# The input LayerNorm of a transformer layer: scale and shift moved behind the transposes, residual rows made later, on one Trainium2 core

## What is computed

```python
def layer_norm(x, g, b):
    mu = jnp.mean(xf, axis=-1, keepdims=True)
    var = jnp.mean(jnp.square(xf - mu), axis=-1, keepdims=True)
    return (xf - mu) * lax.rsqrt(var + LN_EPS) * g + b

h = layer_norm(x, ln_in_g, ln_in_b)
qa, ka, va, qb, kb, vb, ga, gb = jnp.split(h @ w_in, pts, axis=-1)
ya = diff_attention(qa, ka, va, ...)     # branch A, 8 heads
yb = window_attention(qb, kb, vb, ...)   # branch B
merged = sigmoid(ga) * (ya @ w_branch_a) + sigmoid(gb) * (yb @ w_branch_b)
h = layer_norm(ALPHA * h + merged @ w_out, ln1_g, ln1_b)
h = layer_norm(ALPHA * h + square(relu(h @ w_ff1)) @ w_ff2, ln2_g, ln2_b)
```

## Time and profile before

| | |
|---|---|
| median of three runs | 1929.89 us |
| profiled execution, its time | 1934.76 us |
| its span, first to last instruction | 1932.9 us |
| PE busy | 1835.3 us, 95% of the span |
| DVE, ACT, POOL busy | 906.2, 609.7, 504.3 us |
| first matmul of a projection | at 40.09 us |
| first scores of branch A | at 82.93 us |
| branch A, period of a head | 59.5 us |

### The profile page before, as it was taken

How to read it: one execution, slowest core, us unless ns; L and a number is a source line. 1 busy time by engine, 2 the same in 40 slices (tenths; PEclk the granted TensorE clock), 3 DMA queues, 4 the chain that set the end, 5 groups by cost and what they waited for, 6 DMA issues and landing times.

```text
span 1932.9 us, 24565 instructions
## 1 busy us (share of the span) xinstructions
PE 1835.3 (95%) x9174; PEld 1508.9 (78%) x9174; DVE 906.2 (47%) x2051; ACT 609.7 (32%) x1336; POOL 504.3 (26%) x306
## 2 busy tenths in 40 slices
PE   3899999999989998999999999999999999999996
PEld 2777777777768887888888878788888888888884
DVE  7266666676655554111432365434343333334347
ACT  4355555555545555220222221211111111111104
POOL 5111111110113333222221210533222333333224
PEclk9999999999989998999999999999999999999998
DMA  4511111111111100124322350221111111121102
GB/s 161 199 52 32 46 34 34 44 46 33 32 38 31 31 23 23 51 70 138 120 80 66 98 196 1 76 73 48 54 43 43 43 43 43 44 72 47 43 0 87
DMA packets 143109, 117.88 MB, mean 61 GB/s; under 512 B 23285, under 2 KB 129965, under 8 KB 143021
## 3 DMA queue, kind: packets, MB, share of 16 engines
q1 hardware_dynamic: 133804, 112.51, 18.4%
q10 hardware_dynamic: 9216, 4.20, 0.8%
HBM read 99.87 MB, written 21.53 MB: 63 GB/s over the span
## 4 chain that ended last, share of the span: by engine, by line
PE 63%; DVE 4%; ACT 2%; issue 1%; POOL 0%; POOLq 0%; DVEq 0%
PE bank L474 20%; PE bank L475 20%; PE bank L476 20%; ACT mix L866 2%; PE bank L498 1%; DVE mix L1213 1%; PE bank L510 1%; DVE small L1218 1%; DVE res L1095 1%; DVE y_lo L1060 0%; DVE y_lo L1075 0%; ACT y_hi L744 0%; DVE res L1344 0%; ACT y_hi L731 0%; POOL res L964 0%
## 5 line engine op out<-in xcount | busy, mean ns | idle before, releaser
L474 PE MATMUL bank<-hT_hi,w_hi 128*128 128x512 f32 x1312 | 528.7, 403 | 11.6 <-ACT res L750 5.1
L475 PE MATMUL bank<-hT_lo,w_hi 128*128 128x512 f32 x1312 | 516.9, 394 | 0.0
L476 PE MATMUL bank<-hT_hi,w_lo 128*128 128x512 f32 x1312 | 516.7, 394 | 0.0
L959 POOL TENSOR_TENSOR w_lo<-w_raw,w_hi 128x1024 fp32r<-128x1024 f32 x67 | 161.6, 2411 | 710.6 <-ACT w_hi L725 710.5
L474 PEld LDWEIGHTS bank<-hT_hi,w_hi 128*128 128x128 f32 x1312 | 249.6, 190 | 71.9 <-issue 10.2
L476 PEld LDWEIGHTS bank<-hT_hi,w_lo 128*128 128x128 f32 x1312 | 249.7, 190 | 54.2
L475 PEld LDWEIGHTS bank<-hT_lo,w_hi 128*128 128x128 f32 x1312 | 250.0, 191 | 48.8
L474 PE MATMUL bank<-y_hi 128*128 128x512 f32 (+1 forms) x604 | 228.6, 378 | 3.2 <-DVE small L1344 2.6
L475 PE MATMUL bank<-y_lo,y_hi 128*128 128x512 f32 (+1 forms) x604 | 225.8, 374 | 0.0
L476 PE MATMUL bank<-y_hi,y_lo 128*128 128x512 f32 (+1 forms) x604 | 225.8, 374 | 0.0
L1327 DVE TENSOR_TENSOR res<-res,bank 128x512 f32<-128x512 f32 x224 | 154.0, 688 | 141.2 <-PE bank L476 141.2
(11 more groups left out here) (132 smaller groups left out, 2634.5 us busy)
## 6 DMA issues: line engine op xcount, KB each, us to landing
w_raw<-in_w_in_dram SPq DMA_DIRECT2D x100, 256.0 KB, 3.3
w_raw<-in_w_ff_dram SPq DMA_DIRECT2D x64, 256.0 KB, 3.0
mix<-in_w_ff_dram SPq DMA_DIRECT2D x16, 1024.0 KB, 7.2
bias_rows<-bias_line SPq DMA_DIRECT2D x3, 1536.0 KB
res<-in_x_dram SPq DMA_DIRECT2D x8, 512.0 KB, 8.0
h_spill<-res SPq DMA_DIRECT2D x8, 512.0 KB, 6.7
o_spill<-o_buf ACTq DMA_DIRECT2D x64, 64.0 KB, 1.6
w_raw<-in_w_branch_b_dram SPq DMA_DIRECT2D x16, 256.0 KB, 3.9
```

The source lines that it names most:

```text
L474: pe.matmul(bank, lhs[0], rhs[0], start=start, stop=False)
L475: pe.matmul(bank, lhs[0], rhs[1], start=False, stop=False)
L476: return pe.matmul(bank, lhs[1], rhs[0], start=False, stop=stop)
L959: pool.tensor_tensor(w[1][:, n % 2], w_raw[:, :, :], w[0][:, n % 2].bitcast(F32), ALU.subtract).then_inc(w_lo_done, 1)
```

## The change

In the stage ahead of branch A gain and shift are taken out of the rows. A token tile gets only mean and 1/deviation, in one ACT instruction (`normed`: scale 1/deviation, bias -mean/deviation; DVE's `scales` makes the two numbers). PE then transposes not by token tile but by channel block: `turn_tokens(half, kt)` turns four blocks of 128 tokens, one channel block over half the sequence. In that layout gain and shift are one number per partition: DVE applies both while it reads PSUM (`tokens_full`), into one of four slots of `h_full`; ACT rounds it (`tokens_hi`); POOL subtracts (the lo part, no longer DVE). The 16 columns of numbers come from two small loads of 8x128 and one transpose. PE takes the channel blocks into `group(0, half)` one at a time as they are ready, and turns block kt+2 behind block kt. The order of the first four groups becomes (0,0), (1,0), (0,1), (1,1). The subtraction of weight tile 1 goes from POOL to DVE.

The residual rows are made later by POOL (`rows`): behind weight tile n = 2 to 9 it multiplies and adds, two instructions of 128x1024, for token tile n-2. The full rows of gain and shift (0.5 MB each) are loaded behind x instead of after its first tile. Each `h_spill` store waits for its tile (`h_rows`) and stands behind the load of weight tiles 3 to 10; two of the three 1.5 MB transfers of `bias_rows` go behind tiles 4 and 5.

```diff
-for _t in range(NT):
-    BATCHES += [("h0", _t, b) for b in range(2)]
...
@@ sync
-                    sp.dma_start(ln_in[0], row(ln_in_g)).then_inc(ln_in_loaded, 16)
-                    sp.dma_start(ln_in[1], row(ln_in_b)).then_inc(ln_in_loaded, 16)
+                    constants(gb_loaded, (gb_rows[0:KT], by_tile(ln_in_g)), (gb_rows[KT:2 * KT], by_tile(ln_in_b)))
...
-                    for t in range(NT):
-                        sp.wait_ge(ln_done, t + 1)
-                        sp.dma_start(h_spill[t * P:(t + 1) * P, :], res[:, t, :]).then_inc(spilled, 16)
+                if 3 <= n < 3 + NT:
+                    t = n - 3
+                    sp.wait_ge(h_rows, t + 1)
+                    sp.dma_start(h_spill[t * P:(t + 1) * P, :], res[:, t, :]).then_inc(spilled, 16)
+                if n in (4, 5):
+                    repeat_lines(n - 3)
...
@@ tensor
+            def turn_tokens(half, kt):
+                n = half * KT + kt
+                if n >= 2:
+                    pe.wait_ge(h_full_done, n - 1)
+                for t in range(4):
+                    if kt == 0:
+                        pe.wait_ge(ln_done, 4 * half + t + 1)
+                    mm = pe.transpose(TR[n % 2][:, t * P:(t + 1) * P], res[:, 4 * half + t, kt * P:(kt + 1) * P], ident[:, :])
+                mm.then_inc(h_turned, 1)
+            for half in range(2):
+                for kt in range(KT):
+                    pe.wait_ge(h_lo, half * KT + kt + 1)
+                    group(0, half, [kt])
+                    if kt + 2 < KT:
+                        turn_tokens(half, kt + 2)
+                group(1, half, range(4))
+                if half == 0:
+                    for kt in range(2):
+                        turn_tokens(1, kt)
+                group(1, half, range(4, KT))
+            for half in range(2):
+                group(2, half)
...
@@ scalar
+            def normed(t):
+                act.wait_ge(rstd_ready, t + 1)
+                act.activation(res[:, t, :], res[:, t, :], ACT.Identity, bias=neg_mean[:, s:s + 1], scale=rstd[:, s:s + 1]).then_inc(ln_done, 1)
+            def tokens_hi(half, kt):
+                act.wait_ge(h_full_done, n + 1)
+                act.activation(hT[0][:, kt, half * HALF:(half + 1) * HALF], h_full[:, n % 4, :], ACT.Copy).then_inc(h_hi, 1)
+            for kt in range(KT):
+                tokens_hi(0, kt)
+                if kt % 2:
+                    deviation(4 + kt // 2)
+                    if kt > 1:
+                        normed(3 + kt // 2)
+                if kt == 4:
+                    split_weights(1)
...
@@ gpsimd
+                    pool.tensor_tensor(hT[1][:, kt, cols], h_full[:, n % 4, :], hT[0][:, kt, cols].bitcast(F32), ALU.subtract).then_inc(h_lo, 1)
...
+            def rows(t):
+                gain(ln_in[0], t)
+                pool.wait_ge(ln_gain, t + 1)
+                pool.tensor_tensor(res[:, t, :], res[:, t, :], ln_in[1], ALU.add).then_inc(h_rows, 1)
             for n in range(2, TILE[("qb", 1)] + 1):
                 split_weights(n)
+                if n - 2 < NT:
+                    rows(n - 2)
...
@@ vector
+            def tokens_full(half, kt):
+                dve.wait_ge(h_turned, n + 1)
+                if n >= 4:
+                    dve.wait_ge(h_lo, n - 3)
+                dve.tensor_scalar(h_full[:, n % 4, :], TR[n % 2][:, :], gb_cols[:, kt:kt + 1], gb_cols[:, KT + kt:KT + kt + 1],
+                                  ALU.mult, ALU.add).then_inc(h_full_done, 1)
+            for kt in range(KT):
+                tokens_full(0, kt)
+                if kt % 2:
+                    moments_in(4 + kt // 2)
+                    if kt > 1:
+                        scales(3 + kt // 2)
+                if kt == 5:
+                    dve.wait_ge(w_hi_done, 2)
+                    dve.tensor_tensor(w[1][:, 1], w_raw[:, :, :], w[0][:, 1].bitcast(F32), ALU.subtract).then_inc(w_lo_done, 1)
```

More of the change, by code:

```diff
@@ L149, in program @@
         bias_a = aux[1][:, 0:2, :]
-        ln_in = [mix[:, 0, :], mix[:, 1, :]]
+        ln_in = [bias_b_buf[:, :], aux[0][:, 1, :]]
+        gb_rows = mix[0:2 * KT, 2, HALF:HALF + P]
+        gb_cols = small[:, 224:224 + 2 * KT]
+        h_full = mix[:, 0:2, :].rearrange("p s (j q) -> p (s j) q", j=2)
         line_sb = mix[0:A_HEADS + B_HEADS, 2, 0:LINE]
@@ L186, in program @@
         table_loaded = sem("table_loaded")
+        gb_loaded = sem("gb_loaded")
+        gb_turned = sem("gb_turned")
+        gb_ready = sem("gb_ready")
+        h_turned = sem("h_turned")
+        h_hi = sem("h_hi")
+        h_full_done = sem("h_full_done")
+        h_lo = sem("h_lo")
+        rstd_ready = sem("rstd_ready")
+        h_rows = sem("h_rows")
         const_loaded = sem("const_loaded")
@@ L353, in _ @@
             load_weights(1)
+            constants(ln_in_loaded, (ln_in[0], row(ln_in_g)), (ln_in[1], row(ln_in_b)))
             sp.wait_ge(line_sb_done, 1)
@@ L356, in _, with repeat_lines @@
             sp.wait_ge(line_dram, 16)
-            for g in range(3):
+            def repeat_lines(g):
                 sp.dma_start(bias_rows[8 * g:8 * g + 8],
                              bass.AP(bias_line.tensor, 8 * g * LINE, [[LINE, 8], [0, P], [1, LINE]])).then_inc(rows_dram[g], 16)
+            repeat_lines(0)
             def skewed(head, first, n):
@@ L517, in _ @@
             pe.matmul(GEMM[0][0:A_HEADS + B_HEADS, 0:LINE], table, onehot, start=True, stop=True).then_inc(line_done, 1)
[L519 to L532, removed]
+            pe.wait_ge(gb_loaded, 2 * 16)
+            pe.transpose(PV[:, 0:2 * KT], gb_rows, ident[0:2 * KT, 0:2 * KT]).then_inc(gb_turned, 1)
+            def turn_tokens(half, kt):
[8 more added lines that the diff above has]
+            for kt in range(2):
+                turn_tokens(0, kt)
+            pe.wait_ge(line_sb_done, 1)
+            for half in range(2):
[6 more added lines that the diff above has]
+                if half == 0:
+                    for kt in range(2):
+                        turn_tokens(1, kt)
+                group(1, half, range(4, KT))
+            for half in range(2):
+                group(2, half)
             def attend_a(h, i):
@@ L772, in _ @@
             act.wait_ge(eps_ready, 1)
-            for t in range(NT):
-                root(t, t)
+            for t in range(4):
+                deviation(t)
                 if t == 0:
@@ L1095, in norm, with moments_in @@
                 dve.scalar_tensor_tensor(res[:, t, :], res[:, t, :], rstd[:, s:s + 1], shift, ALU.mult, ALU.add).then_inc(ln_done, 1)
[L1097 to L1110 removed]
+            def moments_in(t):
+                dve.wait_ge(x_loaded[t], 16)
+                moments(t, t)
+            for t in range(4):
+                moments_in(t)
+                if t == 1:
+                    dve.wait_ge(gb_turned, 1)
+                    dve.tensor_copy(gb_cols, PV[:, 0:2 * KT]).then_inc(gb_ready, 1)
+                if t:
+                    scales(t - 1)
+            scales(3)
+            dve.wait_ge(gb_ready, 1)
+            for kt in range(KT):
+                tokens_full(0, kt)
[6 more added lines that the diff above has]
+                    dve.tensor_tensor(w[1][:, 1], w_raw[:, :, :], w[0][:, 1].bitcast(F32), ALU.subtract).then_inc(w_lo_done, 1)
+            scales(NT - 1)
+            qk_lo(0, 0)
+            for kt in range(KT):
+                if kt == 2:
+                    qk_lo(1, 0)
+                tokens_full(1, kt)
             dve.wait_ge(const_loaded, 6 * 16)
@@ L1126, in _ @@
             for n in range(2):
-                for half in range(2):
-                    qk_lo(n, half)
+                qk_lo(n, 1)
             def sum_halves(n):
```

89 lines of the change are left out of this document (46 added, 43 removed).

## The result

The changed kernel takes 1941.15 us (median of five runs, 1937.86 to 1941.38). The kernel before, on the same chip in turn with it, takes 1931.53 (1929.71 to 1933.73). The ratio is 1.0045, with a 95% interval of 1.0031 to 1.006: about 9 us slower. The forecast was 1930.3 with a range up to 1936, with "no change" as the likeliest. The measured time lies 5 us above that range.

A forecast was written before the change was run, and what follows sets the result against it. PE, busy for 95% of the span, was taken to bound the kernel. 1934.76 - 7.4 (earlier scores) + 7.8 (waits in heads 0 and 1) = 1935.2, less 4.9 for the median: 1930.3 us, range 1923.5 to 1936.

The forecast's parts named there:

- Part 1: Ahead of branch A: PE's first projection matmul starts at 19.9 us instead of 40.09.
- Part 2: Channel-block loops ahead of branch A: first scores at 75.5 instead of 82.93, a gain of 7.4 us, bounds 2 to 9.
- Part 3: Branch A, heads 0 and 1: POOL's residual-row passes delay DVE, costing PE 7.8 us, bounds 0 to 12.
- i = 2: Heads 0 and 1: L1176 waits for POOL's gain pass, 2.2 late against slack 0.05; PE waits 2.2 us.
- i = 5: Heads 0 and 1: L1174 meets POOL's second pass, L1176 is 2.1 late, slack 0.96; PE waits 1.2 us.
- i = 7: Heads 0 and 1: L1176 starts 1.8 late behind POOL's passes, slack 1.31; PE waits 0.5 us.
- (a): Branch A: DVE is served before POOL's gain pass, saving 4.4 to 8 us; about 1924.5; chance 0.2.
- (c): Branch A: POOL's passes overlap with DVE as if separate, costing under 2 us; 1922 to 1924; chance 0.05.
- (b): Loops ahead of branch A: PE stays at its half rate, costing 7 us; 1937; chance 0.1.
- (d): First channel-block loop takes 24 us rather than 18; 1934 to 1936; chance 0.1.

The follow-up runs named there:

- the filler: Changed kernel with row passes moved to one tile per head in heads 0 to 5, plus ten unused identity transposes ahead of the loops' long waits: 1925.19 us, ratio 0.9972.
- the two single columns: Changed kernel with DVE's 128x2 negation of the maxima split into two 128x1 instructions: 1941.42 us, ratio 1.0063.
- the second experiment: Kernel before with two idle POOL passes of 128x1024 added behind each of weight tiles 4 to 9, nothing else moved: 1943.49 us, ratio 1.0064.
- the first experiment: Changed kernel with POOL's two residual-row passes run over 1 column instead of 1024, stores and transfers kept: 1924.86 us, ratio 0.9969.

## Why the prediction was wrong

**Part 1, the first matmul: right.** Forecast 19.9, measured 20.20. The 20 us of idle wait that went were worth only a few, as said.

**Part 2, the loops: right in kind, 1.5 too good.** The first group ends near 38 as forecast (38.2), group (1,0) at 45.5 instead of 45, group (0,1) at 60.5 instead of 59, and the scores start at 76.98 instead of 75.5. The gain was 5.95, not 7.4. It lies within the bounds of 2 to 9, but one other execution fell below them: in the six kernels with the same two loops (or with the filler) the scores start at 76.98, 77.38, 78.31, 79.27, 79.37 and 81.44, a gain of 1.5 to 6. What differs is how much of the loops ran at the lower clock: the granted clock of the stretch from 20 to 80 us was 0.97 for the first two, 0.94 for the third, 0.91 for the next two and 0.89 for the last. What brings it down in one execution and not in the next is open.

**Part 3, the residual rows: this step failed.** The sum was 3.9 a head and 7.8 in all; measured are 13.2. By its terms:

| term | forecast | measured, head 0 / head 1 | |
|---|---|---|---|
| i = 2 | 2.2 | 2.06 / 2.04 | right, and by L1275 as said |
| i = 5 | 1.2 | 1.31 / 1.26 | right size, wrong cause: the negation L1264 waits |
| i = 7 | 0.5 | 1.29 / 1.28 | wrong: L1264 takes 2.32 and L1273 0.59, L1275 starts 2.5 late and not 1.8 |
| i = 6 | 0 | 0.59 / 0.56 | missing: PE waits for score banks that DVE reads late |
| low clock behind the waits | 0 | 1.65 / 1.19 | missing |

The five lines give 6.90 and 6.33, or 13.2. Three things were missed. First, *which* instruction meets POOL. I had placed the passes correctly, but let only two-tensor instructions be held, so at i = 7 the meeting fell on L1176 (now L1275) with 1.31 of slack, when it was the negation ahead of it that lost 2.15, and L1273 that lost 0.37 more. In the trace of before the negation, L1165, stands at 175.67 and 193.81, just where the forecast put the starts of the gain passes (175.6 and 193.8). That trace held the warning too. L1165 and another one-tensor TENSOR_SCALAR, L1244, both from SBUF to SBUF, each have some executions beside POOL (shortest, median and longest in ns):

```profile
L1165 DVE TENSOR_SCALAR small<-small x64: 168/169/1751, 84.2 to 550.6; 128x2 f32<-128x2 f32 x64
```

```profile
L1244 DVE TENSOR_SCALAR res<-res,small x64: 272/278/2427, 923.4 to 998.6; 128x128 f32<-128x128 f32 x64
```

L1165 took 1.75 at 550.56, beside two POOL memsets; L1244 took 1.7 to 2.4 in seven of its 64 executions, each beside a POOL pass.

What the port cost alone, 10.4 in all, is inside the bounds of 0 to 12; with the clock it is outside.

Second, DVE's lateness doesn't end with the probabilities: what it reads later frees the next score banks later, and PE waits 0.66 at 187.04, one step on.

Third, a wait of 1.2 to 2.4 us can be followed by a stretch at 1.2 GHz, where PE does the same work in up to twice the time; such a wait costs more than its length. The waits as the cause are supported, not proved: of nine profiled executions, the three with new waits over 1 us in heads 0 and 1 (the changed kernel, the passes alone, the two single columns) have low stretches there, and the six others list 1.00 in every window from 70 to 220 us. But it isn't every wait. The one of about 2.4 at i = 2 was followed by a low stretch at four of six places, one of about 1.2 at one of six. A wait of 1.2 that stands at i = 0 of the heads in the kernel before as well (at 150.95, for instance) is followed by none.

The Trainium skill (SBUF — State Buffer, "SBUF: two separate sides") names as what can hold the port pair not only a DVE instruction with two SBUF inputs but also one in a 2-port mode. The Trainium skill (VectorE: DVE Perf Modes, "Mode 2×_2P") says that this mode is for one-source instructions such as `tensor_scalar`, with source and destination in SBUF and an outermost dimension longer than one that is even (or equal on both sides). The runs agree: 128x2 took 2.33 beside POOL and 128x1 took 0.15. I had used the half of the rule that spoke of two inputs. One instruction of the same shape stands apart, the RECIPROCAL L1272 of the changed kernel. It met POOL passes too (at 183.96, in the pass from 182.00 on) and was never held:

```profile
L1272 DVE RECIPROCAL small<-small x64: 165/166/167, 79.3 to 561.8; 128x2 f32<-128x2 f32 x64
```

**The rivals.** (a), DVE slipping past POOL, didn't occur: L1275 at i = 2 came 0.09 behind the gain pass and lost. (c), a port that is no matter, is refuted by the second experiment. (b), the slow rate, was priced as one case of 7 us at the start; it came in pieces of 1 to 4.5 us, in some executions in the loops, and in the two heads behind the new waits, where I hadn't looked for it. (d), the slower first loop, didn't occur.

**The sum against the median.** The forecast took 4.9 off the sum, since the profiled execution of before stood that much above the median. The changed kernel's profiled execution (1941.38) stands 0.2 above its median. The miss of 10.85 us is therefore 1.5 in part 2, 5.4 in part 3 and 4.7 in that offset, less 0.7: the first step of head 0 gains 6.2 and not 5.95, and behind head 2 a shift of 7.1 shrinks to 6.6 of time. The offset goes with the clock. The profiled execution of before has a mean granted clock of 0.987. Of 37 other executions of that kernel beside the experiments, 33 have 0.988 to 0.990; the fastest (1927.38) has 0.991, the two slowest (1935.10, 1935.16) have 0.986. All five of the changed kernel have 0.984 to 0.986. So I subtracted from the forecast what one execution had lost to its clock, while every execution of the changed kernel stands as low or lower. Where those stretches lie in the executions that were not profiled stays open; behind head 2 the two profiled ones list about as many (14 and 11 of some 170 windows below 0.98).

## What to carry to other kernels

Before work is put on POOL, list every DVE instruction of the stretch that has two SBUF inputs or is a one-tensor TENSOR_SCALAR over an even number of columns (2 and 128 here) from SBUF to SBUF, however small, and put the POOL work where none of them is followed by something that PE wants; if no such place exists, cut it in pieces. Here the same passes cost 13.2 us at one place, 4.1 cut in four, and nothing behind the probabilities of step i = 0. A loop in which each block takes a round trip through three engines is paced by that trip over the number of buffers: two more PSUM banks gave about 7 us by the ratios (0.9974 and 0.9938).

## What the runs showed of the hardware

- A DVE TENSOR_SCALAR on 128x2 fp32 numbers, SBUF to SBUF, took 2.33 beside a POOL pass over 128x1024 and 0.17 alone; one on 128x1 took 0.15 beside such a pass. In the prologue of the changed kernel a 128x1 instruction runs beside POOL in the same way, first DVE, then POOL:

```profile
30.75 0.15 DVE L1154 TENSOR_SCALAR small<-small 128x1 f32<-128x1 f32 x1
```

```profile
30.32 1.28 POOL L1036 TENSOR_TENSOR hT_lo<-mix,hT_hi 128x512 fp32r<-128x512 f32 x1 [0.19 <-ACT hT_hi L806]
```

- A DVE RECIPROCAL on 128x2 was not held in any of 64 executions (0.165 to 0.167 us), 12 of them beside POOL; no run shows why.
- The hold lasts one POOL instruction and the waiting DVE instruction gets in before POOL's next: 2.67 beside passes of 1024 columns, 1.05 beside pieces of 256. One place in the trace of before is otherwise: L1165 at 550.56 took 1.75, until the end of the second of two POOL memsets of 0.96 (at 550.44 and 551.33). No run varies that.
- The granted clock fell behind waits of 1.2 to 2.4 us in a stretch that was otherwise nearly all work (0.87 in the window from 140 to 150 us, with PE busy for all of it), and 1.65 and 1.19 us went there; it did so behind some of these waits and not behind others. In the loops ahead of branch A it fell in some executions (0.83 from 50 to 60 us in the first experiment) and not in others of the same loop, the changed kernel's among them.
